# The root and scalings of v ahead of a weight split, and the expert gate's ada product in the routing of the sample

## The chip, the cores and the metric

One Trainium2 chip, one of its cores. The metric is the device time of one execution in microseconds (us). The kernel before takes 1475.08 us, the median of 3 runs (1474.71 to 1475.22).

## The reference

An encoder layer over two sequences, a prompt of 1024 tokens and a sample of 512, with D = 1024. Six rows of modulation come from a product with w_ada: shift, scale and gate of the mixer, shift, scale and gate of the experts. The change touches the last one, gt_f, and the norm of v in the spatial gating.

```python
mod = jax.nn.silu(c) @ w_ada[l] + b_ada[l]
sh_m, sc_m, gt_m, sh_f, sc_f, gt_f = jnp.split(mod, N_MOD, axis=-1)
h = modulate(x, g_mix[l], sh_m, sc_m)
x = x + gt_m[:, None, :] * token_mixer(h, ...)
h = modulate(x, g_ffn[l], sh_f, sc_f)
x = x + gt_f[:, None, :] * expert_choice_moe(h, ...)

# in token_mixer: z = h @ w_in; zb, zc, za, zf, zu, zv = split(z)
v = rms_norm(jax.nn.gelu(zv), g_sgu)
sv = jnp.einsum('hpq,bnqhd->bnphd', w_sp, v) + b_sp.T[None, None, :, :, None]
yc = gelu(zu) * sv

# in expert_choice_moe: 16 experts, cap = 2 * n // 16 tokens each
aff = softmax(hf @ w_router)
gates, idx = lax.top_k(aff.T, cap)
hid = silu(xe @ w_gate) * (xe @ w_up)
ye = (hid @ w_down) * gates
out = zeros.at[idx].add(ye)
```

## The kernel before

Every product in float32 is made from halves of reduced precision: a "hi" part, rounded by ScalarE, and a "lo" part, the remainder, by VectorE. The splits of a weight block stand in both engines' instruction streams, in the order of the code. Each engine runs its stream in order; semaphores tie the engines together, and SP issues nearly all loads.

**Order of the work.** The first ada chunks (shift and scale of the mixer), then the prompt's mixers, its output product in 8 tiles of 128 tokens, the sample's mixers and 4 tiles, the routing, the experts. `z_steps` (L75) lists the steps of the mixers: blocks of W_in (`zf`, `zv`, `zu`, `zc`, `za`, `zb`, three or two of each), the transposes of v (`vt`), the gating (`sv`). For the prompt (s = 0) two ada chunks stand behind each W_in block from `zf1` on, 32 in all: 4 rows of modulation (`ada` 0 to 3: gate of the mixer, shift, scale and gate of the experts) of 8 chunks each. One chunk is 128 rows of w_ada for one modulation row (512 KB); TensorE multiplies it by `silw` in 4 matmuls with 256 columns each.

**The weight stream.** `weight_stream` (L98) is the order in which SP loads W_in blocks, ada chunks, wo blocks and DFT constants, through the three slots of `wraw`. A load waits until its slot's last chunk has been split (`ws_lo`) or multiplied (`ada_used`). ScalarE's `split_ahead` splits the blocks that a step allows and waits for their loads.

**The step zc0.** On both ScalarE (L1083) and VectorE (L2176) the step begins with `split_ahead`; behind it ScalarE takes the root of the mean squares of v (L1090), VectorE inverts it and scales v (`v_norm`, L2109), and TensorE's `gating` (L1628) waits for all 8 scaled tiles (`v_ready`). ScalarE has to load a table of functions ahead of the root.

**PSUM.** The 8 banks are given out ahead of time by `bank_plan` in the order of `bank_events`; `open_bank` on TensorE waits until the bank's last user has been drained. Bank 7 is kept for ada until its last fill. Those products are drained with their bias by VectorE (`ada_drain`, L2039), stored by POOL to `mod_d` in DRAM, and loaded from there as broadcasts to all partitions (`gtm_b`, `shf_b`, `gsf_b`, `gtf_b`).

**The end of the sample's tiles.** In the last tile VectorE's `last_tile` (L2308) computes x2 and h2 and only behind them drains the logits of the two tiles before (`lt_drain`, L2291). TensorE: `router_tokens(1, 1)`, `router_logits(1, 2)`, `router_tokens(1, 2)`, then `first_tokens` (L1732, transposes of the first expert's prompt tokens, eight of them at L1736), `router_blocks(1, 3)` (transposes of h2, L1691), logits, `affinity_rows`. While VectorE runs the sample's top-k, TensorE makes products of the first expert's prompt tokens (`first_high`, `first_low`), then `index_columns(1)` (L1725), 16 transposes that serve only to keep it busy (`keep_clock`), `first_low(3)`, and 8 more. Then come the gathered sample tokens, `first_sample`, and `expert(0, first=4)`; its steps f = 4 to 7 make two products each, and from f = 6 on each waits for VectorE's sum of the step two before. SP loads `gtf_b` from `mod_d` after the last tile (L743). `wait_late` and `load_late` of the diff are new.

Of the kernel before, what the change touches and what calls it, by code (L numbers as in the profile page):

```python
# [19 lines left out]
P = 128  # L20
# [22 lines left out]
N_ADA = 4  # L43
RS, SR = 3, 4
# [35 lines left out]
def z_steps(s):  # L80
# [13 lines left out]
    assert s or ada == N_ADA * KB  # L94
# [22 lines left out]
def bank_events():  # L117
# [117 lines left out]
    job("lt", 1, 2)  # L235
    for k in range(GT):
        opened("xe", k)
# [6 lines left out]
    for n in range(2):  # L244
        opened("cols", n)
# [9 lines left out]
def drainer_of(key):  # L255
# [12 lines left out]
    if name == "out":  # L268
# [4 lines left out]
ADA_HALF = {("adam", 0): 0, ("mod", 0): 1, ("adam", 1): 0, ("mod", 1): 1, ("ada", 0): 0, ("ada", 1): 1, ("ada", 2): 0,  # L273
            ("ada", 3): 1}


def bank_plan(events):
# [4 lines left out]
    for n, (what, key) in enumerate(events):  # L282
# [15 lines left out]
        else:  # L298
            b = min((b for b in range(8) if b not in now_open and (b < 7 or n > last_ada)), key=lambda b: left[b])
# [36 lines left out]
def encoder_kernel(nc, a, y_p, y_s):  # L336
# [40 lines left out]
    rows = at("rows", 196 * K, [P])  # L377
    gtm_b = at("gtm_b", 164 * K, [D])
# [174 lines left out]

    HT_PAIRS = [(0, g, half * 2 + i) for half in range(2) for g in range(NG[0]) for i in range(2)]
# [18 lines left out]
    gtm_in, ffn_in, gtf_in = sems("gtm_in", "ffn_in", "gtf_in")  # L573
# [68 lines left out]
    with nc.Block() as block:  # L642

        @block.sync
        def _(sp):
# [35 lines left out]

            n_next = [0]
# [21 lines left out]
            for s in range(2):  # L704
                stream_until(None if s else ring[first_s])

                wait_filled(sp, "ssq", s, 0)
                for col, dst, arrived in ((2 * D, gtm_b, gtm_in), (3 * D, shf_b, ffn_in)):
# [96 lines left out]
        def _(pool):  # L805
# [7 lines left out]
            for s in range(2):  # L813
                for q in range(2):
                    pool.dma_start(brow_m[2 * 32 * q + s:2 * 32 * q + 64:32, :, :],
                                   a["b_ada"][0, D * q:D * (q + 1)].rearrange("(h c n) -> c h n", h=2, c=2)
                                   ).then_inc(brow_in, 16)
                pool.dma_start(brow_r[s:P:32, :, :], a["b_ada"][0, 2 * D:6 * D].rearrange("(m j n) -> j m n", j=4, n=AW)
# [5 lines left out]
            for j in range(N_ADA):  # L824
                wait_drained(pool, "ada", j)
                for s in range(2):
                    pool.dma_start(mod_d[s, D * (2 + j):D * (3 + j)].rearrange("(j n) -> j n", j=4),
                                   stage_r[s:P:32, j % 2, :]).then_inc(mod_out[j % 2], 16)
# [1930 lines left out]
```

## Time and profile before

| | |
|---|---|
| median of 3 runs | 1475.08 us (1474.71 to 1475.22) |
| the profiled execution | 1476.45 us, its span 1474.6 us |
| TensorE matmul busy | 1430.4 us, 97% |
| VectorE busy | 1031.0 us, 70% |
| ScalarE busy | 727.8 us, 49% |
| GpSimd busy | 164.4 us, 11% |
| chain that ended last | TensorE 86%, VectorE 6%, ScalarE 2%, issue 1%, DMA 1% |
| mean granted clock of TensorE | 0.989 |
| HBM read and written | 288.76 MB and 31.49 MB |

The engine names in the rows are PE (TensorE matmul), PEld (its weight loads), DVE (VectorE), ACT (ScalarE), POOL (GpSimd) and SPq (SP's DMA queue). Matmuls are pipelined and their ends are modelled, so groups overlap by a fraction of a microsecond. All times in rows are counted from the start of the span, which is shorter than the execution's own time by 1.85 us.

### The profile page before, as it was taken

How to read it: one execution, taken by the hardware profiler on the slowest of the kernel's cores; microseconds unless marked ns; L12 is line 12 of the kernel's file. 1: busy time of each engine (PE TensorE's matmuls, PEld its weight loads, DVE VectorE, ACT ScalarE, POOL GpSimd, SP SyncE). 2: the span in 40 equal slices, each digit the busy share in tenths (PEclk: the TensorE clock that was granted, in tenths of full speed). 3: DMA queues.
4: the chain of work that ended last, by engine and by line, in shares of the span. 5: the costliest groups of instructions: out<-in, count | busy, mean ns of one | idle time of the engine just before them, and what ended most of it. 6: DMA issues, size and time to landing. Idle time of an engine off the chain costs nothing.

```text
span 1474.6 us, 22883 instructions
## 1 busy us (share of the span) xinstructions
PE 1430.4 (97%) x8693; PEld 1270.3 (86%) x8693; DVE 1031.0 (70%) x1457; ACT 727.8 (49%) x973; POOL 164.4 (11%) x148
## 2 busy tenths in 40 slices
PE   6999999999999989999999999999999999999994
PEld 4777777888888869999999999999999999999993
DVE  4422533777778888777777777767767777777786
ACT  4422122524542344555555555565565555655663
POOL 1000000000000004002012011012012022011014
PEclk9999999999999989999999999999999999999998
DMA  9333344653421656878778778778778778788796
GB/s 361 119 127 105 112 145 170 201 190 126 154 75 36 221 179 231 255 231 270 260 236 269 257 241 271 246 240 267 249 240 268 249 246 264 246 258 254 251 341 243
DMA packets 187048, 320.94 MB, mean 218 GB/s; under 512 B 7404, under 2 KB 139576, under 8 KB 187000
## 3 DMA queue, kind: packets, MB, share of 16 engines
q1 hardware_dynamic: 178704, 293.89, 58.7%
q0 software_dynamic: 8064, 26.30, 7.1%
q8 instruction: 33, 0.54, 0.1%
q14 instruction: 15, 0.12, 0.0%
q10 hardware_dynamic: 232, 0.09, 0.0%
HBM read 288.76 MB, written 31.49 MB: 217 GB/s over the span
## 4 chain that ended last, share of the span: by engine, by line
PE 86%; DVE 6%; ACT 2%; issue 1%; DMA 1%; POOL 0%; POOLq 0%; SPq 0%; DVEq 0%; ACTq 0%
PE ps L1438 27%; PE ps L1869 25%; PE ps L1867 10%; PE ps L1890 4%; PE ps L1882 4%; PE ps L1891 4%; PE ps L1883 4%; PE ps L1886 4%; PE ps L1872 1%; PE ps L1858 1%; DVE wlo L2296 1%; PE ps L1628 1%; PE ps L1691 1%; ACT whi L1214 1%; DMA accg<-acc_d,iscat 1%
## 5 line engine op out<-in xcount | busy, mean ns | idle before, releaser
L2296 DVE TENSOR_TENSOR wlo<-raw,whi 128x2048 fp32r<-128x2048 f32 x189 | 430.7, 2292 | 181.8 <-ACT whi L1214 181.8
L1869 PE MATMUL ps<-xT,whi 128*128 128x384 f32 x1984 | 557.6, 356 | 0.0
L1867 PE MATMUL ps<-xT,wlo 128*128 128x192 f32 x1736 | 440.5, 254 | 0.0
L1214 ACT ACTIVATE whi<-raw 128x2048 fp32r<-128x2048 f32 x192 | 362.3, 1906 | 0.0
L1869 PEld LDWEIGHTS ps<-xT,whi 128*128 128x128 f32 x1984 | 355.6, 188 | 0.6
L1867 PEld LDWEIGHTS ps<-xT,wlo 128*128 128x128 f32 x1736 | 331.0, 191 | 0.0
L1438 PE MATMUL ps<-hT,wring 128*128 128x512 f32 x1224 | 287.1, 393 | 1.5 <-DVE hT L2081 0.7
L1438 PEld LDWEIGHTS ps<-hT,wring 128*128 128x128 f32 x1224 | 227.2, 188 | 55.1 <-issue 5.9
L1362 ACT ACTIVATE gu_l<-ps 128x384 f32<-128x384 f32 x124 | 60.9, 491 | 185.0 <-PE ps L1869 185.0
L1438 PE MATMUL ps<-wo,Yhl 128*128 128x512 f32 x576 | 135.6, 393 | 0.7 <-DVE wo L2014 0.5
L1438 PEld LDWEIGHTS ps<-wo,Yhl 128*128 128x128 f32 x576 | 106.9, 188 | 23.1 <-issue 0.9
L2014 DVE TENSOR_TENSOR wring<-wraw,wring 128x1024 fp32r<-128x1024 f32 x34 | 41.3, 1220 | 88.3 <-ACT wring L960 88.2
L1340 ACT ACTIVATE hid<-hidf 128x192 fp32r<-128x192 f32 x124 | 45.1, 364 | 104.4 <-DVE hidf L2633 102.4
L1882 PE MATMUL ps<-whi,hid 128*128 128x512 f32 x240 | 94.8, 395 | 0.0
L1890 PE MATMUL ps<-whi,hid 128*128 128x512 f32 x240 | 93.6, 390 | 0.0
L1891 PE MATMUL ps<-wlo,hid 128*128 128x512 f32 x240 | 93.5, 390 | 0.0
L1883 PE MATMUL ps<-wlo,hid 128*128 128x512 f32 x240 | 93.5, 390 | 0.0
L851 POOL DMA_INDIRECT acc_d<-ye,iscat x15 | 24.1, 1608 | 610.8 <-DVE ye L2596 610.8
L960 ACT ACTIVATE wring<-wraw 128x1024 fp32r<-128x1024 f32 x34 | 35.7, 1057 | 90.0 <-DMA wraw<-in_w_in 80.4
L2626 DVE TENSOR_TENSOR gu<-ps,gu_l 128x384 f32<-128x384 f32 x124 | 68.6, 553 | 16.4 <-ACT gu_l L1362 16.4
L1886 PE MATMUL ps<-whi,hid 128*128 128x512 f32 x240 | 73.9, 389 | 0.0
L1872 PE MATMUL ps<-xT,wlo 128*128 128x192 f32 x248 | 62.5, 252 | 0.0
(279 smaller groups left out, 1598.5 us busy)
## 6 DMA issues: line engine op xcount, KB each, us to landing
raw<-in_w_gate SPq DMA_DIRECT2D x64, 1024.0 KB, 5.3
raw<-in_w_up SPq DMA_DIRECT2D x64, 1024.0 KB, 5.8
raw<-in_w_down SPq DMA_DIRECT2D x64, 1024.0 KB, 5.1
wraw<-in_w_in SPq DMA_DIRECT2D x34, 512.0 KB, 5.6
wraw<-in_w_ada SPq DMA_DIRECT2D x32, 512.0 KB, 4.6
ada_w<-in_w_ada SPq DMA_DIRECT2D x16, 512.0 KB, 13.0
acc_d<-x SPq DMA_DIRECT2D x12, 512.0 KB, 2.7
h_d<-h SPq DMA_DIRECT2D x12, 512.0 KB, 3.9
```

What stands on the lines that cost most here:

```text
L1214: act.activation(whi[:, slot_at(j), :], raw[:, j % RAW, :], ACT.Copy).then_inc(w_hi, 1)
L1438: return pe.matmul(out, lhsT, rhs, start=start, stop=stop, skip_group_check=True)
L1867: pe.matmul(out[:, 0:CAP], wlo[:, slot, w], xT[:, k, 0:CAP], start=False, stop=False, skip_group_check=True)
L1869: mm = pe.matmul(out[:, 0:2 * CAP], whi[:, slot, w], xT[:, k, :], start=k == 0, stop=k == KB - 1, skip_group_check=True)
L1872: pe.matmul(out[:, 0:CAP], wlo[:, slot, w], xT[:, k, 0:CAP], start=False, stop=False, skip_group_check=True)
L1882: pe.matmul(ps[:, 4 + n, :], hid[:, f, part[0]], whi[:, slot_at(8 + k), w], start=start, stop=False)
L1883: pe.matmul(ps[:, 4 + n, :], hid[:, f, part[0]], wlo[:, slot_at(8 + k), w], start=False, stop=False)
L1886: pe.matmul(ps[:, 4 + n, :], hid[:, f, part[1]], whi[:, slot_at(8 + k), w], start=False, stop=stop)
L1890: pe.matmul(ps[:, 6 + n, :], both, whi[:, slot_at(8 + k), w], start=start, stop=False)
L1891: mm = pe.matmul(ps[:, 6 + n, :], both, wlo[:, slot_at(8 + k), w], start=False, stop=stop)
L2296: dve.tensor_tensor(wlo[:, slot_at(j), :], raw[:, j % RAW, :], whi[:, slot_at(j), :].bitcast(F32), ALU.subtract).then_inc(w_split, 1)
L2626: dve.tensor_tensor(gu[:, f % 2, :, :], ps[:, b:b + 2, 0:CAP], gu_l[:, f % 2, :, :], ALU.add).then_inc(gu_summed, 1)
```

## The change

It does two things. First, at the step zc0 the root of ScalarE and `v_norm` of VectorE are put in front of `split_ahead`. Second, the expert gate's ada product (chunks 24 to 31) leaves the first sequence. Its 8 chunks, `late_ada`, stand in TensorE's stream in four pairs: behind `router_tokens(1, 2)`, behind `first_tokens`, ahead of `first_high(0)`, and behind `index_columns(1)`, where `keep_clock` falls from 16 to 6 transposes. They collect in the upper half of bank `cols` 1, which is opened early. SP loads them into slots 1 and 2 of `wraw`: 0 and 1 behind the first four raw chunks of the experts, 2 and 3 at the last tile ahead of its wait for h2, 4 to 7 behind the tiles; from chunk 2 on each waits until the chunk two before has been used. VectorE adds the bias (`gstage`) behind `first_sample_sum(0)`; POOL, not SP, stores it to `mod_d`, waits for that, and loads `gtf_b`. The activated c moves in `silw` from columns 0 and 1 to 16 and 17, so that the router's weights don't overwrite it. SP's waits for `mod_out` ahead of `gtm_b` are new. The bank plan shifts by one user from zb2 on.

```diff
@@ z_steps
-            for _ in range(2 if s == 0 and blocks >= len(FIRST) else 0):
+            for _ in range(2 if s == 0 and blocks >= len(FIRST) and ada < N_EARLY_ADA * KB else 0):
@@ bank_plan
-            b = min((b for b in range(8) if b not in now_open and (b < 7 or n > last_ada)), key=lambda b: left[b])
+            b = min((b for b in range(5 if key == ("cols", 1) else 0, 8) if b not in now_open and (b < 7 or n > last_ada)),
+                    key=lambda b: left[b])
@@ encoder_kernel
+    LATE_ADA = N_EARLY_ADA * (KB - 1)
+
+    def wait_late(eng, m):
+
+        loads = len(range(1 + m % 2, len(stream), RS)) + m // 2 + 1
+        eng.wait_ge(ws_in[1 + m % 2], 16 * loads)
@@ SP
+            def load_late(m):
+
+                if m >= 2:
+                    sp.wait_ge(ada_used, LATE_ADA + m - 1)
+                sp.dma_start(wraw[:, 1 + m % 2, :], w_ada[P * m:P * (m + 1), 5 * D:6 * D]).then_inc(ws_in[1 + m % 2], 16)
...
                     for j in range(RAW):
                         load_chunk(sp, 0, j)
+                    sp.wait_ge(ws_lo, len(splits))
+                    wait_filled(sp, "odd", 1, 1)
+                    load_late(0)
+                    load_late(1)
...
+                    if tt == NT - 1:
+                        load_late(2)
+                        load_late(3)
                     sp.wait_ge(h2_ready, tt + 1)
...
-            sp.wait_ge(prompt_in, 4)
-            for s2 in range(2):
-                sp.dma_start(gtf_b[:, s2, :], mod_d[s2:s2 + 1, 5 * D:6 * D].to_broadcast([P, D])
-                             ).then_inc(gtf_in, 16)
+            for m in range(4, KB):
+                load_late(m)
@@ GpSimd
+            pool.wait_ge(gtf_staged, 1)
+            for s in range(2):
+                pool.dma_start(mod_d[s, 5 * D:6 * D].rearrange("(j n) -> j n", j=4), gstage[NE + s:P:32, :]).then_inc(mod_out[1], 16)
+            pool.wait_ge(mod_out[1], 64)
+            for s in range(2):
+                pool.dma_start(gtf_b[:, s, :], mod_d[s:s + 1, 5 * D:6 * D].to_broadcast([P, D])).then_inc(gtf_in, 16)
             pool.wait_ge(routed, 7)
@@ ScalarE, mixers
-                    if kind in COL:
-                        split_ahead(("wi", s, kind, i))
                     if (kind, i) == ("zc", 0):
                         act.wait_ge(var_v, s + 1)
...
+                    if kind in COL:
+                        split_ahead(("wi", s, kind, i))
@@ TensorE
+            def late_ada(part):
+
+                for m in part:
+                    wait_late(pe, m)
+                    for j in range(4):
+                        ins = mm(bank("cols", 1)[32 * j:32 * (j + 1), AW:2 * AW], silw[:, m, :],
+                                 wraw[:, 1 + m % 2, AW * j:AW * (j + 1)], m == 0, m == KB - 1)
+                    ins.then_inc(ada_used, 1)
...
             router_tokens(1, 2)
+            open_bank("cols", 1)
+            late_ada(range(0, 2))
             first_tokens()
+            late_ada(range(2, 4))
             router_blocks(1, 3)
...
             open_bank("xe", GT)
-            for n in range(2):
-                open_bank("cols", n)
+            open_bank("cols", 0)
+            late_ada(range(4, 6))
             pe.wait_ge(prompt_lo, 4)
...
             index_columns(1)
-            keep_clock(16, "cols", 1)
+            late_ada(range(6, 8))
+            keep_clock(6, "xe", 2)
@@ VectorE, mixers
                 for n, (kind, i) in enumerate(z_steps(s)):
+                    if (kind, i) == ("zc", 0):
+                        v_norm(s)
                     if kind in COL:
                         split_ahead(("wi", s, kind, i))
                     if kind == "ada" and i % KB == KB - 1:
                         ada_drain(i // KB)
-                    if (kind, i) == ("zc", 0):
-                        v_norm(s)
@@ VectorE, first expert
             first_sample_sum(0)
+            dve.wait_ge(ada_used, LATE_ADA + KB)
+            dve.wait_ge(brow_in, 16 * 8)
+            dve.tensor_tensor(gstage[:, :], bank("cols", 1)[:, AW:2 * AW], brow_g[:, :], ALU.add).then_inc(gtf_staged, 1)
             split(0, 6)
```

## Rows read from the trace of the kernel before

**Rows 1.** Timeline, TensorE: start, length, engine, line, operation, count, idle before.
```profile
155.17 1.07 PE L1438 MATMUL ps<-wraw,silw 128*32 128x256 f32 x16
...
158.67 7.13 PE L1628 MATMUL ps<-wspT,v 128*64 128x128 f32 x96 [2.43 <-DVE v L2116]
```
**Rows 2.** Timeline, ScalarE and VectorE, around the step zc0.
```profile
142.90 1.09 ACT L1106 ACTIVATE Y<-ps 128x512 f32<-128x512 f32 x2 [3.92 <-PE ps L1438]
153.04 1.06 ACT L960 ACTIVATE wring<-wraw 128x1024 fp32r<-128x1024 f32 x1 [9.05 <-DMA wraw<-in_w_in]
154.12 1.28 ACT L1090 ACT_TABLE_LOAD   x1
...
155.89 2.73 DVE L2116 TENSOR_SCALAR v<-v,ssv 128x384 f32<-128x384 f32 x8
```
**Rows 3.** Stretches: PE, PEld, DVE, ACT, POOL busy, clock, DMA share, GB/s.
```profile
160.00:161.00 1.00, 1.00 (x14) 1.00 (x12) 0.97 (x2) 0.00 (x0) 0.34 (x1) 0.50 0.99 406
```
**Rows 4.** Timeline, TensorE, gating of the second sequence.
```profile
436.67 2.84 PE L1628 MATMUL ps<-wspT,v 128*64 128x128 f32 x48
```
**Rows 5.** Timeline, TensorE, an ada pair and the W_in block behind it.
```profile
239.33 1.07 PE L1438 MATMUL ps<-wraw,silw 128*32 128x256 f32 x16
240.33 11.21 PE L1438 MATMUL ps<-hT,wring 128*128 128x512 f32 x48
```
**Rows 6.** Timeline, VectorE and then TensorE, end of the first mixers.
```profile
264.76 0.42 DVE L2044 TENSOR_TENSOR stage_r<-ps,brow_r 128x256 f32<-128x256 f32 x1
265.10 7.26 DVE L2244 SCALAR_TENSOR_TENSOR Yhl<-Y,VT,Yhl 128x1024 fp32r<-128x1024 f32 x6
...
282.31 3.00 PE L1438 MATMUL ps<-wo,Yhl 128*128 128x512 f32 x12 [0.47 <-DVE wo L2014]
```
**Rows 7.** Timeline, TensorE, routing of the sample.
```profile
539.15 0.85 PE L1736 MATMUL ps<-ident_sb,xp 128*128 128x128 f32 x6
544.07 0.69 PE L1736 MATMUL ps<-ident_sb,xp 128*128 128x128 f32 x2 [4.07 <-DVE L L2291]
544.55 1.92 PE L1691 MATMUL ps<-ident_sb,h 128*128 128x128 f32 x8
...
565.36 0.20 PE L1725 MATMUL ps<-ident_sb,vals 16*64 16x16 f32 x1 [1.26 <-DVE idxf L2473]
```
**Rows 8.** Timeline, VectorE, the drains of the logits in the last tile.
```profile
543.77 0.25 DVE L2291 COPY L<-ps 128x16 f32<-128x16 f32 x2
```
**Rows 9.** Stretches around the wait of 4.07 us.
```profile
540.00:544.00 4.00, 0.00 (x1) 0.00 (x0) 3.71 (x9) 3.72 (x8) 0.00 (x0) 0.76 0.00 0
544.00:548.00 4.00, 3.64 (x26) 2.40 (x26) 3.80 (x6) 1.80 (x7) 0.00 (x0) 0.50 0.84 293
```
**Rows 10.** Line L673: landing of an ada pair issued at 131.6, then W_in at 246.0.
```profile
DMA to landing us min/median/max: 3.7/4.1/4.6
...
DMA to landing us min/median/max: 3.2/3.2/3.2
```
**Rows 11.** Landing of L735's store at 510.8; ScalarE's timeline; a step of the chain.
```profile
DMA to landing us min/median/max: 6.6/6.6/6.6
...
519.88 1.25 ACT L1236 ACTIVATE x<-ps,rsy 128x512 f32<-128x512 f32 x2
...
522.88 0.72 DVE x L2368 x2
```
**Rows 12.** Landing of POOL's stores to mod_d (L827), then of its gathers (L839).
```profile
DMA to landing us min/median/max: 1.9/3.2/5.6
...
DMA to landing us min/median/max: 4.5/5.2/6.0
```
**Rows 13.** Timeline, VectorE, first expert.
```profile
577.12 0.68 DVE L2614 TENSOR_TENSOR tot<-ps,sl 64x512 f32<-64x512 f32 x1 [1.56 <-ACT sl L1303]
...
586.57 0.55 DVE L2626 TENSOR_TENSOR gu<-ps,gu_l 128x384 f32<-128x384 f32 x1
```
**Rows 14.** Timeline, TensorE, last matmul of f = 5 and first of f = 6.
```profile
589.64 0.54 PE L1869 MATMUL ps<-xT,whi 128*128 128x384 f32 x2
```

More of the change, by code:

```diff
@@ L43 @@
 N_ADA = 4
+N_EARLY_ADA = 3
 RS, SR = 3, 4
@@ L90, in z_steps @@
             blocks += 1
-            for _ in range(2 if s == 0 and blocks >= len(FIRST) else 0):
+            for _ in range(2 if s == 0 and blocks >= len(FIRST) and ada < N_EARLY_ADA * KB else 0):
                 out.append(("ada", ada))
                 ada += 1
-    assert s or ada == N_ADA * KB
+    assert s or ada == N_EARLY_ADA * KB
     return out
@@ L235, in bank_events @@
     job("lt", 1, 2)
+    opened("cols", 1)
     for k in range(GT):
@@ L270, in drainer_of @@
     return "act" if name in ("zc", "zf", "zu", "zv", "vt", "lg", "even") else "dve"
-ADA_HALF = {("adam", 0): 0, ("mod", 0): 1, ("adam", 1): 0, ("mod", 1): 1, ("ada", 0): 0, ("ada", 1): 1, ("ada", 2): 0,
-            ("ada", 3): 1}
+ADA_HALF = {("adam", 0): 0, ("mod", 0): 1, ("adam", 1): 0, ("mod", 1): 1, ("ada", 0): 0, ("ada", 1): 1, ("ada", 2): 0}
 def bank_plan(events):
@@ L377, in encoder_kernel @@
     rows = at("rows", 196 * K, [P])
+    gstage = at("gstage", 196 * K, [AW])
+    brow_g = at("brow_g", 197 * K, [AW])
     gtm_b = at("gtm_b", 164 * K, [D])
@@ L707, in _ @@
                 wait_filled(sp, "ssq", s, 0)
+                for i in range(2):
+                    sp.wait_ge(mod_out[i], 32 * (2 - i))
                 for col, dst, arrived in ((2 * D, gtm_b, gtm_in), (3 * D, shf_b, ffn_in)):
@@ L823, in _ @@
                                a["b_spatial"][0, h:h + 1, :].to_broadcast([HD, P])).then_inc(bsp_in, 16)
-            for j in range(N_ADA):
+            for j in range(N_EARLY_ADA):
                 wait_drained(pool, "ada", j)
@@ L827, in _ @@
                     pool.dma_start(mod_d[s, D * (2 + j):D * (3 + j)].rearrange("(j n) -> j n", j=4),
-                                   stage_r[s:P:32, j % 2, :]).then_inc(mod_out[j % 2], 16)
-            wait_filled(pool, "ada", N_ADA - 1)
+                                   stage_r[NE + s:P:32, j % 2, :]).then_inc(mod_out[j % 2], 16)
+            wait_filled(pool, "ada", N_EARLY_ADA - 1)
             pool.dma_start(silw[:, :, 0:NE], a["w_router"][0].rearrange("(k p) n -> p k n", p=P)).then_inc(wrt_in, 16)
@@ L887, in _ @@
                                  ).then_inc(first_copied, 1)
+            pool.wait_ge(gtf_staged, 1)
+            for s in range(2):
+                pool.dma_start(mod_d[s, 5 * D:6 * D].rearrange("(j n) -> j n", j=4), gstage[NE + s:P:32, :]).then_inc(mod_out[1], 16)
+            pool.wait_ge(mod_out[1], 64)
+            for s in range(2):
+                pool.dma_start(gtf_b[:, s, :], mod_d[s:s + 1, 5 * D:6 * D].to_broadcast([P, D])).then_inc(gtf_in, 16)
             pool.wait_ge(routed, 7)
@@ L1837, in _ @@
             open_bank("xe", GT)
-            for n in range(2):
-                open_bank("cols", n)
+            open_bank("cols", 0)
+            late_ada(range(4, 6))
             pe.wait_ge(prompt_lo, 4)
@@ L2511, in mod_drain @@
                 drain(dve.tensor_copy(modT[:, half, :, :, :], ada_bank("mod", half).rearrange(
-                    "p (m j n) -> p m j n", m=2, j=4)[:, :, :, 0:2]), "mod", half)
+                    "p (m j n) -> p m j n", m=2, j=4)[:, :, :, NE:NE + 2]), "mod", half)
                 wait_drained(dve, "mod", half)
```

21 lines of the change are left out of this document (13 added, 8 removed).

## The prediction

> **What bounds the kernel now.** I read the page first (shares, the chain that ended last): TensorE is busy 97% of the span, so a change pays where TensorE itself works less, or where a wait of TensorE goes. Then the list of what TensorE waited for, and for each wait that the change touches the timelines of the engines around it. There are three places.
>
> (a) First sequence, ahead of the gating: TensorE ends an ada pair at 156.24, then stands 2.43 us until the scaled v is there [rows 1]. ScalarE drained the last zu at 143.99, then stood 9.05 us in the split of the next weight block, whose load was not there; only behind it came the root (with a table load), and behind that VectorE's scalings, eight in 2.73 us [rows 2]. Behind the wait TensorE's granted clock is 0.50, the lower level of 1.2 GHz, in three slices of 1 us, the first of which is shown [rows 3]. (b) From there to the end of the last block of W_in, zb2, TensorE has no wait; blocks and ada pairs stand end to end, one of them in [rows 5]. (c) Last tile of the sample: TensorE waits 4.07 us, up to VectorE's drain of the logits, and from there a chain without slack runs through it: transposes of h2, logits, softmax, the rounds of the top-k, the indices [rows 7, 8]. The clock is 0.50 here too [rows 9].
>
> **The change, part by part.**
>
> *Root and scalings first.* ScalarE can begin with the table load at 143.99; from that load to the first scaling it was 155.89 - 154.12 = 1.77, and the scalings take 2.73 [rows 2], so they end at about 148.5, some 7.7 us before TensorE asks. The wait of 2.43 goes. What is late next: the split of the next block, whose load ends it at 153.04 as before; that block is used only behind the gating, at 165.7. With no standstill in front of it the gating should keep the full clock. It took 7.13 for 96 matmuls; at full clock in the second sequence 48 took 2.84, of which about 0.07 is the tail of the last one, so 96 take 5.55 [rows 1, 4]. That is 1.6 more. **Part: -4.0** (-2.4 if the clock falls all the same). In the second sequence TensorE doesn't wait there: nothing.
>
> *Ada chunks 24 to 31 leave the first sequence.* A pair costs 1.00 from its start to that of the next block (239.33 to 240.33) [rows 5]. Three pairs (behind zb1, zc2 and za2) stand between full blocks: -3.0. The fourth, behind zb2, runs while VectorE's chain sets the end of this stage (TensorE waits for a wo split of VectorE at 282.31 [rows 6]): nothing of it counts but its drain on VectorE, which stands in that chain, 0.34 between 264.76 and 265.10 [rows 6]: -0.3. With fewer loads in the stream the splits come no later: a block of 11.2 now needs two loads in place of four. **Part: -3.3.** Cover lost: none.
>
> *Chunks 0 and 1 behind the router of tile 2.* They need bank 5, whose last user is lt(1,1). VectorE drains that only after the last tile's h2, with the first of the two copies at 543.77 [rows 8]. So they do not lie in the wait of 4.07: they start when it ends, at about 544.0. The six transposes that ran at 539.15, ahead of the wait, now stand behind it too [rows 7]. At the lower clock [rows 9] a chunk costs at most twice its 0.5, so chunk 0 ends at about 545.0 and chunk 1 at 546.0.
>
> *Chunks 2 and 3 between first_tokens and the transposes of h2.* SP may issue the load of chunk 2 only when chunk 0 has been used, and that of chunk 3 only after chunk 1, since only two slots are free. So the loads go out at 545.15 and 546.15. A load of this kind took 3.7 (the first of a pair) and 4.6 (the second); one alone, of W_in, 3.2 [rows 10]. That gives landings at 548.4 to 548.9 and 549.4 to 550.7. I take 3.8 for both, being nearest to the first of a pair of the same tensor: 549.0 and 550.0. Chunk 2 is done at 550.0, chunk 3 at 551.0. TensorE is in order, and the transposes of h2 that began at 544.55 [rows 7] begin at 551.0. **Part: +6.4**, all on the chain; from 549.9 to 551.7 it is +5.3 to +7.1. Queued behind: VectorE's drain of h2T and its low parts of the prompt's tokens, ScalarE's drain and its Exp; all of them shift as one. SP's stores of the last tile go out behind the loads, some 2.5 later; the gather of the sample, first to need them, stands behind the indices.
>
> *Chunks 4 to 7.* Chunks 4 and 5 stand ahead of first_high. TensorE waits 1.26 for the indices at 565.36 [rows 7]. At the lower clock they take 2.0, but the same length of other work then falls into the full clock at half its time, so the net is 1.0, inside the 1.26. Six and seven take the place of ten keep-clock transposes behind the indices, of about the same length together. Both: 0, at most +0.5. SP waits for each of them ahead of the expert's raw chunk 4, whose load then goes out later against the chain, but still while the top-k runs; its split stands behind the indices. Nothing.
>
> *Loads 0 and 1* are queued behind four raw chunks, ahead of the stores of the sample's first tile. 1.05 MB more at 293 GB/s (a stretch with much traffic [rows 9]) is 3.6 us, and puts the landing of that store from 510.8 + 6.6 = 517.4 to 521.0. ScalarE writes the same x2 buffer from 519.88 to 521.13, so 1.1 late, and VectorE reads it only at 522.88 [rows 11]: nothing, with 0.6 to spare.
>
> *The gate's rows.* VectorE adds the bias behind first_sample_sum(0), which ends at 577.8 [rows 13], in a wait for ScalarE: staged at 578.3. POOL then stores both rows (1.9 to 5.6 to landing, median 3.2 [rows 12]), the second half a us behind the first, which gives 582.0, and issues two broadcasts of 512 KB. Nearest rows are its gathers of the same size under the same load: 4.5 to 6.0 [rows 12]. The second lands at 582.7 + 5.2 = 587.9 (bounds 585.4 and 590.5). VectorE now waits for it ahead of expert 0 (586.57 before [rows 13]), which makes it 1.3 late. What is behind it is the sum for f = 4, and TensorE needs that at f = 6, from about 589.9 [rows 14]; the sum takes 0.55, so landings up to 589.3 cost nothing. **Part: 0**, at most +1.2. Queued behind on POOL: the gather of expert 1, some 10 us later than before; TensorE needs it only in the middle of the down products of expert 0. Nothing. All of these times lie in the frame of the kernel before. The Trainium skill ("DMA: Bandwidth & Descriptors", Anatomy of one DMA) gives 2.0 us plus bytes at 436 GB/s for a DMA issued from GpSimd: an estimate of 3.2 for each broadcast. By it the part is 0 as well, with more room, but the gathers here took longer, and I go by them.
>
> **Sum:** -4.0 - 3.3 + 6.4 + 0 = -0.9. The profiled execution took 1476.45 (span 1474.6): it becomes 1475.5. The median of the runs is 1475.08, which gives **1474.2**.
>
> **The rivals.**
>
> *A, the chain waits longer (slower than before).* Place: chunk 3's load and the broadcasts. If the loads land at the upper end (+7.1), TensorE comes late to the indices (+0.5) and the broadcasts land at 590.5 (+1.2), the sum is +1.5; with the clock low in the gating all the same, +3.1. It decides from a landing of the broadcasts after 589.3, each us counting fully. For it: two waits for DMAs on the chain where there were none. Against: the DMA engines move nothing from 540 to 544 [rows 9]. Time 1476.6 to 1478.2.
>
> *B, the clock comes back early.* From 544 to 548 TensorE was busy 3.64 of 4 us, nearly all of it with transposes, and stayed at 0.50 [rows 9]. With chunks 0 to 3, true matmuls, in this stretch, the upper level of 2.4 GHz could return before the transposes of h2. Chunk 3 would then cost 0.5 less, the transposes of h2 0.9, the logits 0.4 and the transposes of the softmax 0.5 less: -2.3 in all. Time 1471.9. For it: the stretch holds four chunks more of work. Against: it is cut by a wait of 1 to 2 us. The Trainium skill ("TensorE: Matmul & The Clock Gate", Part 4: PE-mode transpose) says that transposes don't count as TensorE being busy in the way of other matmuls; the trace agrees with it at 544 to 548, but doesn't show what matmuls in their place would do.
>
> *C, chunks 2 and 3 don't hold the chain* (the loads find their slots earlier than I read, or the transposes get ahead). Then only chunks 0 and 1 and the six transposes count, at most +3.3: time 1471.1. Against: the order on TensorE and the semaphore counts are fixed in the code.
>
> *D, the change doesn't do what it says:* the split stands with the wait, and v is scaled late all the same; -4.0 falls away, time 1478.2. Against: nothing but the split stands in front of the root in ScalarE's order.
>
> **How the numbers follow.** Forecast 0.58; A 0.17; B 0.15; C 0.06; D 0.04. The forecast's own terms give 1473.1 (a fast load) to 1475.4. The range of 8 in 10 takes in B and the lower half of A: 1471.8 to 1477.4. Of this kernel a measurement can tell about 0.2%, 3 us, so faster means under 1472.1 and slower over 1478.0: faster holds over half of B and all of C, 0.15; slower holds the upper end of A and most of D, 0.10; the rest, 0.75, is no difference.
>
> **What the profile after would show.** No wait ahead of the 96 gating matmuls, their group at 5.6, granted clock 1.00 there; 24 ada chunks in the first sequence; the first tile of the output product some 7.3 earlier. TensorE waits about 1.3 to 3 us for a DMA into wraw behind first_tokens, and the span from the last drain of logits in the last tile to the indices is 6 us longer. If that stretch isn't longer, C or B is right; if VectorE's wait ahead of expert 0 is over 3 us and TensorE stands ahead of f = 6, A. I am wrong in the whole if the first part gives less than 6, since everything else rests on the two nearly cancelling.

## The result and the profile after

The changed kernel takes 1476.56 us, the median of 13 runs (1475.59 to 1477.71); the kernel before, on the same chip, 1474.48 us (1471.81 to 1476.79). The ratio is 1.0016, 95% interval 1.0009 to 1.0023: some 2.4 us slower (2.1 us between the medians), where 0.9 us faster was forecast. The time lies inside the range. The profiled execution took 1477.33 us, its span 1475.5.

The page of the changed kernel, its span, busy times and the chain that ended last by engine:
```profile
span 1475.5 us, 22870 instructions
## 1 busy us (share of the span) xinstructions
PE 1429.7 (97%) x8683; PEld 1268.9 (86%) x8683; DVE 1030.7 (70%) x1457; ACT 728.4 (49%) x973; POOL 169.0 (11%) x153
...
PE 88%; DVE 5%; DMA 3%; SPq 1%; ACT 1%; issue 1%; POOL 0%; POOLq 0%; DVEq 0%; ACTq 0%
```
Busy times of TensorE, VectorE and ScalarE are as before, and SP's queue and DMAs have a larger part in the chain: work has only changed places, and the question is what waits were traded. First the gain. These are timelines of the changed kernel (start, length, engine, line, operation, count, idle before), ScalarE and VectorE, then TensorE around the gating of sequence 1; they answer to [rows 1, 2].
```profile
144.64 1.28 ACT L1122 ACT_TABLE_LOAD   x1
...
153.39 1.06 ACT L994 ACTIVATE wring<-wraw 128x1024 fp32r<-128x1024 f32 x1 [7.25 <-DMA wraw<-in_w_in]
...
146.41 2.73 DVE L2164 TENSOR_SCALAR v<-v,ssv 128x384 f32<-128x384 f32 x8
...
155.80 1.07 PE L1472 MATMUL ps<-wraw,silw 128*32 128x256 f32 x16
156.80 5.46 PE L1671 MATMUL ps<-wspT,v 128*64 128x128 f32 x96
```
The table load and the scalings end while ScalarE still waits for the next block, and the gating starts right behind the ada pair, in 5.46 us. Then the loss, the changed kernel's TensorE in the last tile, which answers to [rows 7]:
```profile
536.44 1.94 PE L1472 MATMUL ps<-wraw,silw 128*32 128x256 f32 x16 [4.71 <-DVE L L2339]
538.31 1.97 PE L1779 MATMUL ps<-ident_sb,xp 128*128 128x128 f32 x8
541.38 1.08 PE L1472 MATMUL ps<-wraw,silw 128*32 128x256 f32 x8 [1.10 <-DMA wraw<-in_w_ada]
544.28 1.08 PE L1472 MATMUL ps<-wraw,silw 128*32 128x256 f32 x8 [1.83 <-DMA wraw<-in_w_ada]
545.30 1.97 PE L1734 MATMUL ps<-ident_sb,h 128*128 128x128 f32 x8
...
565.71 0.20 PE L1768 MATMUL ps<-ident_sb,vals 16*64 16x16 f32 x1 [0.47 <-DVE idxf L2521]
```
VectorE's drain of the logits ends the long wait as before, but 9.08 us now lie between its start (536.22) and the transposes of h2; before it was 544.55 - 543.77 = 0.78 [rows 7, 8]. Two chunks, eight transposes, a wait for chunk 2, chunk 2, a wait for chunk 3, chunk 3 stand in between.

How the two balance is read from the starts of the same instructions, in timelines of TensorE. "Before again" is a second profiled execution of the kernel before, the first experiment below.

| start of, us | before | before again | scalings first | after |
|---|---|---|---|---|
| gating, sequence 1 | 158.67 | 158.40 | 156.34 | 156.80 |
| the W_in block behind it | 165.73 | 163.79 | 161.74 | 162.19 |
| output tile that waits for wo | 282.31 | 280.42 | 278.32 | 274.80 |
| gating, sequence 2 | 436.67 | 434.79 | 432.68 | 429.15 |
| transposes of h2, last tile | 544.55 | 542.66 | 540.53 | 545.30 |
| transposes of the indices | 565.36 | 563.48 | 561.34 | 565.71 |
| first product of f = 4, expert 0 | 580.00 | 578.13 | 575.98 | 580.35 |

### The profile page after: what moved, and what is told of

It is laid out like the page before. It is cut to its first block, busy times and chain, and to the rows that moved or that the text cites. A ratio compares the mean times of both kernels' runs of the same rounds, so it can differ in the third digit from the quotient of the medians.

```text
span 1475.5 us, 22870 instructions
## 1 busy us (share of the span) xinstructions
PE 1429.7 (97%) x8683; PEld 1268.9 (86%) x8683; DVE 1030.7 (70%) x1457; ACT 728.4 (49%) x973; POOL 169.0 (11%) x153
## 4 chain that ended last, share of the span: by engine, by line
PE 88%; DVE 5%; DMA 3%; SPq 1%; ACT 1%; issue 1%; POOL 0%; POOLq 0%; DVEq 0%; ACTq 0%
PE ps L1472 28%; PE ps L1916 25%; PE ps L1914 10%; PE ps L1937 4%; PE ps L1929 4%; PE ps L1938 4%; PE ps L1930 4%; PE ps L1933 4%; PE ps L1919 1%; DMA ada_w<-in_w_ada 1%; PE ps L1905 1%; DVE wlo L2344 1%; PE ps L1734 1%; ACT whi L1248 1%; DMA acc_d<-x 1%
```

## The experiments

The kernels were timed in three groups, each beside the kernel before on the same chip, which took 1473.77 us (33 runs, 1471.67 to 1476.26) with before again, scalings first, chunks 2 and 3 later and stores held back; 1473.95 (28 runs) with the scalings undone, the gate's wait moved, all chunks in waits and the early bank alone; 1473.81 (21 runs) with the last two kernels. I compare ratios to it; a difference of two ratios is given in us of some 1474.

**The kernel before again** (no edit).

> The kernel before, unchanged, timed and traced once more. The two traces at hand differ by 0.9 us in their spans, the medians of 13 runs by 2.1. Theory 1 (the profiled execution of before was a long one, and what it had more lies in the first 60 us, where transfers of ada_w set the pace): the ratio is 1.000 within 0.001, and the new trace differs from the old by 1 to 3 us, all of it ahead of the first block of W_in at 63.3. Theory 2 (the difference lies elsewhere): stages behind that point differ between the two traces of the same kernel.

It took 1473.98 us, ratio 1.0002 (0.9993 to 1.0011). Its TensorE at the gating:
```profile
158.40 5.46 PE L1628 MATMUL ps<-wspT,v 128*64 128x128 f32 x96 [1.80 <-DVE v L2116]
```
and the stretches of the profiled execution of before, then of this one (us, TensorE busy, granted clock, DMA share, GB/s):
```profile
158.00:162.00 4.00, 3.33 (x42) 0.72 0.86 337
...
158.00:162.00 4.00, 3.60 (x66) 1.00 0.95 358
```
The wait is shorter, and the clock did not fall behind it: 5.46 in place of 7.13. So two executions of one kernel are 1.7 us apart in the clock and 0.6 in a wait. My reading that all of the difference between them stands ahead of 63 us was wrong. The prediction took the one execution that it had as the typical one.

**Two more profiled executions of the kernel before** (no edit), later, to see how often.

> The kernel before, unchanged, one more profiled execution. Theory (the clock falls behind the wait ahead of the gating of sequence 1 in some executions only): either the gating takes 7.1 us with the granted clock at 0.72 to 0.85 in 158 to 166, or 5.5 us at 1.00, and the wait is 1.8 to 2.4 us; two of three looks so far (this kernel again, and the changed one with the scalings undone) showed 5.5. Rival (the fall is the rule and the other looks were chance): 7.1.

> As the look before: 5.5 us or 7.1 us for the gating of sequence 1, and the wait ahead of it 1.8 to 2.4 us.

TensorE's gating in the first and in the second of them:
```profile
156.84 5.46 PE L1628 MATMUL ps<-wspT,v 128*64 128x128 f32 x96 [0.49 <-DVE v L2116]
...
158.69 5.46 PE L1628 MATMUL ps<-wspT,v 128*64 128x128 f32 x96 [2.52 <-DVE v L2116]
```
No fall in either, not even behind 2.52 us. The wait itself moves between 0.49 and 2.52, outside what I expected (1.8 to 2.4). The execution with the short one took 1471.83 us, that with the long one 1474.71; 1.8 of these 2.9 us are there at the block behind the gating (162.24 and 164.08), the rest arises later. What moves the wait is the load that ScalarE's split waits for; ScalarE in the first and in the second:
```profile
151.21 1.06 ACT L960 ACTIVATE wring<-wraw 128x1024 fp32r<-128x1024 f32 x1 [7.11 <-DMA wraw<-in_w_in]
...
153.06 1.06 ACT L960 ACTIVATE wring<-wraw 128x1024 fp32r<-128x1024 f32 x1 [9.14 <-DMA wraw<-in_w_in]
```

**Root and scalings first, alone**, on the kernel before.
```diff
                 for n, (kind, i) in enumerate(z_steps(s)):
-                    if kind in COL:
-                        split_ahead(("wi", s, kind, i))
                     if (kind, i) == ("zc", 0):
                         act.wait_ge(var_v, s + 1)
...
+                    if kind in COL:
+                        split_ahead(("wi", s, kind, i))
...
+                    if (kind, i) == ("zc", 0):
+                        v_norm(s)
                     if kind in COL:
                         split_ahead(("wi", s, kind, i))
...
-                    if (kind, i) == ("zc", 0):
-                        v_norm(s)
```


> The kernel before with the root and the scalings of v ahead of the split, and nothing else of the change. My theory: the wait of 2.43 us goes and the gating group falls from 7.13 to 5.5 at the full clock, so 4.0 us less than before. Rival: the gain is given back where the output product waits for VectorE, and the time is that of before within 1 us. Second rival: only the wait goes, 2.4 less.

1472.02 us (1471.17 to 1472.47), ratio 0.9989 (0.9980 to 0.9998): 1.75 less between the medians. Against before again it is 2.05 ahead at the block behind the gating, and keeps that to the first expert (575.98 against 578.13). So the second rival is nearest: the part works as described and is worth its wait, not its wait and the clock. The runs spread over 1.3 us only, where those of the kernel before spread over 4.6, but that doesn't show the wait to be what varied: the early bank below has no wait there either and spreads over 4.5, the next kernel has it and spreads over 1.6.

**Root and scalings back behind the split, in the changed kernel** (the edit above, reversed).

> The changed kernel with the root and the scalings of v put back behind the split. Theory (the parts add up): 1.9 us more than the changed kernel, that is some 4 us more than the kernel before; the wait of about 2 us ahead of the gating is back in the trace, and the gating of sequence 1 takes 5.5 us, or 7.1 in an execution in which the clock falls behind the wait. Rival (with three pairs of chunks gone from the blocks ahead of it, the order of VectorE's and ScalarE's work around the first x gates has changed and the wait has gone or grown): a wait under 1 or over 3 us, and a time that differs from the changed kernel's by less than 1 or more than 3 us.

1478.30 us, ratio 1.0029 (1.0018 to 1.0040), against 1.0016 for the changed kernel: 1.9 more, as expected, though the intervals overlap. The wait ahead of the gating is back with 1.67 us, and the clock does not fall. As far as the runs can tell, the part is worth the same with and without the other.

**Chunks 2 and 3 behind the last tile's router tokens**, in the changed kernel.
```diff
             first_tokens()
-            late_ada(range(2, 4))
             router_blocks(1, 3)
             router_logits(1, 3)
             router_tokens(1, 3)
+            late_ada(range(2, 4))
```


> The changed kernel with chunks 2 and 3 behind the sample's last router tokens, where TensorE waits for the softmax, in place of ahead of the transposes of h2. My theory (the chain waited for their loads): the transposes of h2 begin about 5 us earlier than in the changed kernel; but chunks 4 and 5 then wait for their own loads ahead of first_high, up to 3 us, so TensorE reaches the indices late and 2 to 4 us of the 5 remain, 2 to 4 under the changed kernel. Rival (the chain was held by chunks 0 and 1 and by the moved transposes): less than 1 us under the changed kernel.

1474.38 us, ratio 1.0004 (0.9995 to 1.0013): 1.8 less than the changed kernel. The transposes of h2 begin at 539.71, 5.2 sooner than after against the gating of sequence 2, the indices at 563.01, 2.3 sooner. More than half of the gain is lost to a wait further on, TensorE behind the softmax:
```profile
548.52 2.28 PE L1472 MATMUL ps<-wraw,silw 128*32 128x256 f32 x16 [2.85 <-DMA wraw<-in_w_ada]
```
The loads of chunks 4 and 5 may go out only when 2 and 3 have been used. With two slots, a chunk that is used later makes a load later.

**The last tile's stores held back** until chunk 3 has been used.
```diff
                         load_late(3)
+                        sp.wait_ge(ada_used, LATE_ADA + 4)
```


> The changed kernel, with SP holding the two stores of the last tile until chunk 3 has been used. In the changed kernel the load of chunk 3 took 5.8 us, with 1 MB of stores issued 0.4 us behind it, and that of chunk 2 took 3.8. My theory (the stores share the DMA engines with the load): the load of chunk 3 takes 3.8 to 4.2, the transposes of h2 begin 1.6 to 2 us earlier, and the time is 1.6 to 2 under the changed kernel. Rival (the 5.8 comes from the load itself, or from chunk 2's being in flight): it stays over 5 us and the time is that of the changed kernel.

1475.64 us, ratio 1.0012 (1.0003 to 1.0021): 0.6 less than the changed kernel, where 1.6 to 2 were expected, and within the intervals, so the runs don't show a gain. The traces show more. SP's queue and the landing of chunk 3's load (issued at 538.44), in the changed kernel:
```profile
537.59 1.19 SPq L696 DMA_DIRECT2D wraw<-in_w_ada  x2
538.82 0.43 SPq L760 DMA_DIRECT2D acc_d<-x  x1
539.29 0.43 SPq L761 DMA_DIRECT2D h_d<-h  x1
...
DMA to landing us min/median/max: 5.8/5.8/5.8
```
and here, where the stores are issued only at 542.88:
```profile
537.14 1.19 SPq L696 DMA_DIRECT2D wraw<-in_w_ada  x2
542.88 0.33 SPq L761 DMA_DIRECT2D acc_d<-x  x1
...
DMA to landing us min/median/max: 4.1/4.1/4.1
...
540.66 0.64 PE L1473 MATMUL ps<-wraw,silw 128*32 128x256 f32 x8 [0.93 <-DMA wraw<-in_w_ada]
542.18 0.64 PE L1473 MATMUL ps<-wraw,silw 128*32 128x256 f32 x8 [0.88 <-DMA wraw<-in_w_ada]
542.75 1.87 PE L1735 MATMUL ps<-ident_sb,h 128*128 128x128 f32 x8
```
Without the two stores (1 MB) that SP issues 0.4 and 0.9 us behind it, the load landed 1.7 us sooner. The transposes of h2 come 2.1 us sooner; 0.4 of that is the clock, at 1.00 from 540 to 542 here (0.64 in place of 1.08 for a chunk).

These are single executions, and the figure moves. Three more kernels of this document issue the stores as closely behind the load of chunk 3, and there it took 5.3 us (scalings undone), 6.2 (chunks 2 and 3 later) and 6.6 (gate's wait moved). This is the last of them, TensorE at chunk 3 and the landing:
```profile
544.75 1.08 PE L1472 MATMUL ps<-wraw,silw 128*32 128x256 f32 x8 [3.16 <-DMA wraw<-in_w_ada]
...
DMA to landing us min/median/max: 6.6/6.6/6.6
```
In the four kernels below with the early bank, which issue the stores some 3.5 us behind that load, it took 4.7, 4.7, 5.5 and 5.8, of which SP's issuing instruction itself took 0.4 to 1.4. So 5.3 to 6.6 with stores right behind the load stand against 4.1 to 5.8 without. The ranges overlap: that the stores delay the load is likely, by how much is not settled.

**The wait for the gate's rows moved to their first use**, in the changed kernel.
```diff
+                    if first:
+                        dve.wait_ge(gtf_in, 32)
                     outputs(e)
...
-            dve.wait_ge(gtf_in, 32)
             expert(0, first=FIRST_F)
```


> The changed kernel, but VectorE waits for the broadcast of the expert gate's rows only before the first expert's outputs, where they are first used, and no longer at the head of the first expert. Theory (the gate's rows cost a little): VectorE's 2.8 us of wait at the head of expert 0 goes, and with it TensorE's 0.3 us behind it, so 0.2 to 0.5 us less than the changed kernel. Rival (the wait is hidden, the queue work is the cost, or there is none): the same time as the changed kernel within 0.1 us.

1476.75 us, ratio 1.0018 (1.0009 to 1.0027): no less than the changed kernel, as the rival said, though the runs can't tell 0.2 us from nothing. VectorE's first sum of expert 0, in the changed kernel and in this one:
```profile
589.77 0.56 DVE L2674 TENSOR_TENSOR gu<-ps,gu_l 128x384 f32<-128x384 f32 x1 [2.77 <-DMA gtf_b<-mod_d]
...
587.43 0.55 DVE L2674 TENSOR_TENSOR gu<-ps,gu_l 128x384 f32<-128x384 f32 x1
```
The wait is gone, and no gain shows. From the first product of f = 4 to the last instruction of VectorE it is 883.35 us here, 883.34 with the wait in the kernel of the scalings undone, and 884.04 in the changed one; the last two differ by more than the wait could.

**All chunks in waits**, in the changed kernel (with the edit just shown).
```diff
+            open_bank("cols", 1)
             router_tokens(1, 1)
             router_logits(1, 2)
             router_tokens(1, 2)
-            open_bank("cols", 1)
             late_ada(range(0, 2))
             first_tokens()
-            late_ada(range(2, 4))
             router_blocks(1, 3)
             router_logits(1, 3)
             router_tokens(1, 3)
+            late_ada(range(2, 4))
...
-            late_ada(range(4, 6))
             pe.wait_ge(prompt_lo, 4)
             first_high(0)
             first_low(0)
             for j in range(1, 4):
                 first_high(j)
+            late_ada(range(4, 6))
```


> The changed kernel with its late chunks where TensorE stands still: chunks 0 and 1 ahead of the wait of 4.7 us for the last router logits (their bank is opened earlier), chunks 2 and 3 behind the last tile's router tokens, 4 and 5 behind the first products of expert 0, 6 and 7 as they were; the gate's wait as in the run before. Theory (the gain of the first two parts, 1.9 and 4.0 us, is there, and the routing took it back through where the chunks stood and how late their loads came): the h2 transposes come some 6.9 us sooner against the gating of sequence 2 than in the changed kernel, the transposes of the indices 5 to 6.9 us sooner, the whole 5 to 7.5 us less than the changed kernel, that is 3 to 5.5 us less than the kernel before. Rival (the chunks cost what they cost wherever they stand, since each holds TensorE or one of its queues): at most 2 us less than the changed kernel, so no faster than before.

A miss: 1476.25 us, ratio 1.0011 (1.0002 to 1.0020), hardly less than the changed kernel. That is the rival's figure, but not for its reason: the chunks do cost less where they stand. Counted from the start of the span, the transposes of h2 begin at 536.15 and the indices at 557.16, 9.2 and 8.6 sooner than after; the first product of f = 4 begins at 580.29, and all but 0.1 is lost. SP, ScalarE and TensorE in this kernel:
```profile
553.86 0.80 SPq L696 DMA_DIRECT2D wraw<-in_w_ada  x2
555.11 0.40 SPq L650 DMA_DIRECT2D raw<-in_w_gate  x1
...
563.17 1.91 ACT L1248 ACTIVATE whi<-raw 128x2048 fp32r<-128x2048 f32 x1 [6.04 <-DMA raw<-in_w_gate]
...
569.60 1.12 PE L1984 MATMUL ps<-ident_sb,hid 128*128 128x128 f32 x4 [3.82 <-DVE hid L2657]
```
Chunks 4 and 5 are used at 553.16, 1.3 later than in the changed kernel, although the chain around them runs some 9 sooner. So the loads of 6 and 7 are issued at 553.9 as there, and the expert's weights stand behind them in SP's queue, at 555.1. ScalarE waits 6.04 us for these weights, its next sigmoid stands behind that split, and TensorE waits for the hidden values made from it.

**The early bank alone**: only the first edit of the kernel above, so chunks 0 and 1 run ahead of the wait for the logits.
```diff
+            open_bank("cols", 1)
             router_tokens(1, 1)
             router_logits(1, 2)
             router_tokens(1, 2)
-            open_bank("cols", 1)
             late_ada(range(0, 2))
```


> The changed kernel with only the bank of the late chunks opened earlier, so that chunks 0 and 1 run inside the 4.7 us for which TensorE waits for the last router logits, and the loads of chunks 2 and 3 are issued some 4.5 us sooner, ahead of the last tile's stores. Theory: the h2 transposes come 4.9 us sooner against the gating of sequence 2, since both waits for chunks 2 and 3 (1.1 and 1.8 us) go too and the two chunks cost 1.9 us at the low clock; the whole 3.5 to 5 us less than the changed kernel. Rival (VectorE's chain of the top tokens takes over as the bound, as behind the second experiment, where 5.2 us at the h2 transposes became 2.7 at the indices): 5 us less at the transposes, but 2 to 3 us in the whole.

1470.18 us (1467.88 to 1472.33), ratio 0.9971 (0.9962 to 0.9981): 6.6 less than the changed kernel, where 3.5 to 5 were expected, and 4.3 less than the kernel before, the fastest of all. TensorE:
```profile
531.75 1.07 PE L1472 MATMUL ps<-wraw,silw 128*32 128x256 f32 x16
532.75 1.09 PE L1779 MATMUL ps<-ident_sb,xp 128*128 128x128 f32 x8
535.95 1.08 PE L1472 MATMUL ps<-wraw,silw 128*32 128x256 f32 x8 [2.11 <-DMA wraw<-in_w_ada]
537.57 1.08 PE L1472 MATMUL ps<-wraw,silw 128*32 128x256 f32 x8 [0.54 <-DMA wraw<-in_w_ada]
538.58 1.97 PE L1734 MATMUL ps<-ident_sb,h 128*128 128x128 f32 x8
```
Chunks 0 and 1 and the transposes of the tokens run at the full clock inside what was the wait. The wait for chunk 2 now lies inside it too, and only 0.54 for chunk 3 is left behind the drain of the logits (536.28). The transposes of h2 come 6.8 sooner than after against the gating of sequence 2, more than the 4.9 that I had worked out, in which the tokens' transposes had stayed behind the logits. The gain is not cut at the indices (559.44, 6.3 sooner).

**The early bank, with chunks 2 and 3 behind the router tokens** (both edits shown above, chunks 4 to 7 where the changed kernel has them).

> The kernel of the early bank, with chunks 2 and 3 put behind the last tile's router tokens, as in the second experiment; chunks 4 to 7 where the changed kernel has them. That is the kernel with all chunks in waits, less the move of chunks 4 and 5 (and less the gate's wait, which moved nothing). Theory (what spoiled that kernel was SP's queue: its loads of chunks 6 and 7 were issued at 553.9 instead of 546.9, and the expert's weights behind them at 555.1 instead of 548.5, so the conversions waited 6.0 us): the weights are issued by 549 again, the wait of 3.8 us for hid is gone, and since the loads of chunks 4 and 5 now come later TensorE waits some 2.5 us for them, so that the h2 transposes come 2.4 us sooner than with the early bank alone and the indices at the same time within 1 us; the whole 0 to 1 us less than with the early bank alone (1469 to 1470.5). Rival (chunks 2 and 3 behind the tokens are what spoiled it): 4 to 6 us more than with the early bank alone.

1471.03 us, ratio 0.9982 (0.9973 to 0.9991). Against all chunks in waits it is 4.3 less: the weights are issued at 549.07, and the 3.8 us for the hidden values are gone. That chain, set off by where chunks 4 and 5 stood, was the cause. Against the early bank alone it is 1.6 more by the ratios, where 0 to 1 less was expected; the intervals overlap. TensorE waits for chunk 4:
```profile
546.00 2.23 PE L1472 MATMUL ps<-wraw,silw 128*32 128x256 f32 x16 [2.28 <-DMA wraw<-in_w_ada]
```

**Chunks 4 and 5 behind the first products of expert 0**, in that kernel.
```diff
-            late_ada(range(4, 6))
             pe.wait_ge(prompt_lo, 4)
             first_high(0)
             first_low(0)
+            late_ada(range(4, 6))
```


> The kernel of the run before, with chunks 4 and 5 behind the first high and low products of expert 0 (some 4 us of TensorE's work), where their loads have landed. Theory: TensorE no longer waits for those loads, so the transposes of the indices come when VectorE's chain of the top tokens ends, some 2 us sooner than with the early bank alone; SP issues the expert's weights no more than 1 us later than there, so the gain stays: 1 to 2.5 us less than with the early bank alone (1467.5 to 1469). Rival (any delay of the weights behind the chunks' loads is paid in full at the conversions): the same as the early bank alone or up to 2 us more.

1470.81 us, ratio 0.9977 (0.9968 to 0.9986): no less than the early bank alone (0.9 more, intervals overlapping), so the rival's figure. The wait for chunk 4 is gone and the indices come at 557.42, 2.0 sooner than with the early bank alone, but the first product of f = 4 only 0.5. Behind the indices stands a wait that was not there, TensorE for the gathered tokens, and ScalarE waits 0.63 and 1.07 us for weights:
```profile
557.42 0.20 PE L1768 MATMUL ps<-ident_sb,vals 16*64 16x16 f32 x1 [1.79 <-DVE idxf L2521]
...
563.67 0.63 PE L1850 MATMUL ps<-ident_sb,xe 128*128 128x128 f32 x4 [0.79 <-DMA xe<-h_d,icur]
```
The gather took 5.2 us to land here and 3.5 with the early bank alone. That the sooner indices bring it among SP's loads of weights is my reading of the times; no run here moved those loads.

## Why the prediction was wrong

By its own steps, with before again as the kernel before, since that execution lies near the median:

| part | predicted | measured | from |
|---|---|---|---|
| root and scalings first | -4.0 | -1.9 | start of the block behind the gating, less the 0.3 by which this execution starts later; runs -1.75 and -1.9 |
| chunks out of the first sequence | -3.3 | -4.0 | 280.42 - 163.79 = 116.63 becomes 274.80 - 162.19 = 112.61 |
| routing up to the transposes of h2 | +6.4 | +8.3 | 542.66 - 434.79 = 107.87 becomes 545.30 - 429.15 = 116.15 |
| from there to the first product of f = 4 | 0 | -0.4 | 35.47 becomes 35.05 |
| gate's rows | 0 | 0 | moving the wait gave no gain |
| sum | -0.9 | +2.0 | runs +2.1 to +2.4 |

Of the 2.9 between the sums, 2.1 come from the first part and 1.9 from the third, and the other two give back 0.7 and 0.4. Two terms were mis-sized, and either alone would have left the sum within 1.2 of nothing. The third and fourth rows hold for these two executions: the routing term is 7.7 by the trace of the scalings undone and 9.1 by that of the gate's wait moved, and the stretch behind it takes 34.84 to 35.78 in the four executions of the kernel before, so its -0.4 is not clear of them.

**Part 1: the mechanism right, the term mis-sized by 2.1.** "The wait of 2.43 goes" held, and the gating has 5.46 as against 5.55 forecast. Two figures failed, both because one execution was taken for the kernel. The clock's 1.6 was in 1 of 5 profiled executions with the scalings behind the split; the prediction had "-2.4 if the clock falls all the same", but the case that counted was that the clock does not fall before either. And the wait is 0.49 to 2.52, in the mean of those five 1.8. The working scaled a sum made against the profiled execution to the median by a fixed distance (1.4 us); the distance itself held one of the terms. The spread of the three runs given, 0.5 us, could not show that, the later ones show 5. The Trainium skill ("TensorE: Matmul & The Clock Gate", Part 1: The HAM clock gate) calls it run-variable how many matmuls run at the lower level before the clock rises at a kernel's start. Here it is the fall behind a wait that varies, four gatings at 5.46 and one at 7.13. The first tile of the output product did begin 7.5 sooner than in the execution that the prediction had (282.31 and 274.80, forecast 7.3), but only 5.6 sooner than in before again (280.42).

**Part 2: right, 0.7 too small.** A pair costs more than the 1.00 between its start and the next block's: the block ahead of it runs for 11.14 until the pair starts (240.33 to 251.47), where blocks without pairs follow each other at 10.92. In the kernel before, the block behind the one of [rows 5] starts 12.14 us after it:
```profile
252.47 11.22 PE L1438 MATMUL ps<-hT,wring 128*128 128x512 f32 x48
```
In the chain of the changed kernel four blocks without pairs take 10.92 each:
```profile
212.69 43.69 PE ps L1472 x192
```
So a pair costs 1.22, three 3.66, and with the drain's 0.34 it is 4.0. The last pair was rightly not counted: TensorE's wait for the wo split, 0.47 [rows 6], is 1.52 now.
```profile
274.80 2.97 PE L1472 MATMUL ps<-wo,Yhl 128*128 128x512 f32 x12 [1.52 <-DVE wo L2062]
```

**Part 3: one step failed, the landing of chunk 3's load, mis-sized by 2.0.** Counted from the drain of the logits, chunk 2 starts at 5.16 (forecast 5.23) and chunk 3 at 8.06 (forecast 6.23). Its load was issued at 2.22 (forecast 2.38) and took 5.8 us instead of "3.8 for both"; that is the whole 1.85 by which the stage was underestimated. The prediction had 4.6 for the second load of a pair [rows 10] and took the first one's 3.8 for both; that is 0.8 of it. (The lower end of its +5.3 to +7.1 is also 0.5 too low: a landing at 549.4 and a chunk of 1.0 make 550.4.) For the rest, it says that the stores "go out behind the loads, some 2.5 later", and asks only who waits for the stores, not what they do to the load in flight. With them held back the load took 4.1, with them right behind it 5.3 to 6.6 in four executions; the runs' 0.6 us doesn't settle how much of this is theirs. The Trainium skill ("DMA: Bandwidth & Descriptors", Queues, rings and completion order) says that on each DMA engine descriptors are consumed in ring order, but carry no barrier, so that a later one may finish its write before an earlier one. It gives no time for a load with stores behind it, and through what they would delay the load no run here shows.

**Chunks 4 to 7: right.** The wait for the indices fell from 1.04 in before again (1.26 in the execution that the prediction had) to 0.47, and what is behind the transposes of h2 grew by nothing that shows.

**Loads 0 and 1: right.** The store behind them landed 9.1 us after its issue at 504.42, and ScalarE's write of the same buffer came 1.12 late, forecast 1.1:
```profile
513.57 1.27 ACT L1270 ACTIVATE x<-ps,rsy 128x512 f32<-128x512 f32 x2 [1.12 <-DMA acc_d<-x]
```
It cost nothing: from the gating of sequence 2 to the drain of the logits it is 536.22 - 429.15 = 107.07, and was 543.77 - 436.67 = 107.10.

**The clock in the routing.** It came back ahead of the softmax:
```profile
548.00:552.00 4.00, 1.61 (x18) 0.90 (x22) 2.57 (x11) 3.25 (x4) 0.00 (x0) 0.93 0.14 53
```
That is 3 us too late for the transposes of h2, which still took 1.97 at the low level, and it doesn't show rival B's mechanism. The kernel before, which has no chunks there, also gets the clock back behind these transposes in two of four profiled executions; this is the second of the later two:
```profile
547.00:549.00 2.00, 0.12 (x2) 0.08 (x2) 1.24 (x6) 1.99 (x3) 0.00 (x0) 1.00 1.00 205
```
With the gate's wait moved, where the routing is that of the changed kernel, the clock was at 1.00 from 540 to 542 already, an early return like B's, but at 0.50 again from 543 on, so the transposes of h2 took 1.97 there too.

**The gate's rows: the sum right, the length wrong.** VectorE is held 2.77 us, not 1.3, because the two broadcasts took longer than the gathers that I went by (4.5 to 6.0 [rows 12]), 6.5 and 7.5 us:
```profile
DMA to landing us min/median/max: 6.5/7.0/7.5
```
TensorE waits 0.3 us on its weight loads for VectorE's sum, and moving the wait brought no gain that the runs or the traces show. The Trainium skill ("DMA: Bandwidth & Descriptors", Anatomy of one DMA) would give an estimate of 3.2 us for each; the trace is at more than double, so here the page is too low.

**The rivals.** A had the right sign and the right load, which landed even later than its upper end, but two of its three terms were empty: the broadcasts cost nothing and TensorE was not late for the indices. C and D fell: the chunks hold the chain, and the wait ahead of the gating is gone. The bound that I had set for being wrong in the whole, "if the first part gives less than 6", was met: the first two parts gave 5.9. What the list of rivals lacked was the case "the profiled execution is not the median one, in just this stretch".

## What to carry to other kernels

Where a term is a wait that a load ends, or a fall of the clock behind one, look whether it is there in more than one execution before it enters the sum at full size; with one profile, take it as a range that reaches to nothing. When work is moved into a wait, follow the bank or slot that lets it start: here two edits that freed 5.9 us ahead of it came out slower than before, until a bank was opened three calls earlier. And follow what stands behind the moved loads in the same queue: with chunks 4 and 5 used late, the expert's weights went out at 555.1 in place of 549.1, and TensorE stood 3.8 us for it.

## What the runs showed of the hardware

The same wait ahead of the same 96 matmuls lowered the granted clock once (behind 2.43 us) and did not in four other profiled executions (behind 2.52, 1.80, 1.67 and 0.49). A load of 512 KB issued 0.4 us ahead of two stores of 512 KB on the same queue landed in 5.3 to 6.6 us in four executions; without stores that close behind it, in 4.1 to 5.8 in five. Two broadcasts of 512 KB each issued by GpSimd, beside the expert's weights, took 6.5 and 7.5 us.
